# Fourier stages of a two-block kernel: the context's output product placed ahead of the latents', and half of the latents' gate product moved to GpSimd

## The chip, the cores and the metric

The kernel runs on one core of a Trainium2 chip, as one launch. The metric is the device time in microseconds (us), the median over several runs. Engines are named as the profile names them: PE is TensorE (PEld its weight loads), DVE is VectorE, ACT is ScalarE, POOL is GpSimd, SP is SyncE. L3534 is line 3534 of the kernel before.

## The reference

Two transformer-like blocks follow each other on 1024 latent positions and 256 context positions of width 1024. The first (latent attention, a chunkwise mLSTM, a mixture of 16 experts) isn't touched. The second has two layers; each projects its input into parts, runs attention, a Fourier branch, a convolution and a pooling branch, and projects the concatenation with `w_out`. The Fourier branch is:

```python
def _fourier_branch(u, z, w_fourier):
    b, n, _ = u.shape
    uf = u.astype(jnp.float32).reshape(b, n, F_HEADS, F_DIM)      # F_HEADS = 4, F_DIM = 64
    y = jnp.fft.fftn(uf, axes=(1, 3), norm='ortho').real.reshape(b, n, W_F).astype(u.dtype)
    return jax.nn.silu(z) * (y @ w_fourier)                       # W_F = 256
```

In the first layer it is computed for the latents (n = 1024) and for the context (n = 256). In the second layer only the latents' result is needed.

## The kernel before, in words

`layer` (L3723 on) is called for l = 0 and 1. Each layer projects its input, runs attention, then `fourier` (L3386 on, called once per layer), then `project_out`. Everything lies with the 128 partitions as channels and the positions along the row: `g.parts` holds the projected parts, and `g.o[j]`, j = 0 and 1, the two groups of 128 output channels of the Fourier branch. A row has the 256 context positions first and the 1024 latent ones behind them.

The transform along the positions uses symmetry. The input is folded into a sum and a difference of its two halves (`fold`, L3495), turned by TensorE's transposes (L3424), multiplied with a cosine and a sine table (`transform`, L3433), and then multiplied with the combined head transform and `w_fourier` (`w2`). This last stage is called `leave` on TensorE and on VectorE. For each j it gives an even and an odd part, of `half` columns each (512 for the latents, 128 for the context); position t is even plus odd, position n - t is even minus odd. The middle position has products of its own, of one column each (`middle`, and the first loop of `leave`).

There are no planners here: each engine runs a list written out by hand, with semaphores between the lists, within one block (L3394). All engines meet at a barrier at the block's end, before `project_out` starts. The lists before the change, from the point that the change touches:

- TensorE (L3452 to L3472): latents turned and transformed (cosines, `middle`, sines); in layer 0 the context turned and transformed (L3459 to L3464); waits for the latents' spectrum (`cos_out`, `sin_out`, `mid_done`); `leave` of the latents (L3468), which raises `out_full` once per j; in layer 0 waits for the context's spectrum (`cos_out` 3, `mid_done` 2) and `leave` of the context (L3472), which raises `out_full` to 3 and 4.
- ScalarE: copies of the sines' spectrum (L3484), then the odd part of each j out of PSUM (L3487), which raises `odd_done`.
- VectorE: in layer 0 the context's spectrum (`spectra`, L3521), then `leave` of the latents for j = 0 and 1, then of the context for j = 0 and 1. One `leave` is five steps: the middle column (L3526), the odd part (a wait for ScalarE, or for the context a copy, L3530), even plus odd (L3531), even minus odd written backwards (L3532), and the product of the whole row with the gate `z` (L3534). The helper `Steps` lets VectorE wait for each of its own steps before the next.
- GpSimd: four small copies in layer 0, two in layer 1 (L3403), and nothing behind them in this block.
- SyncE: one load of `w_out` (L3397).

`project_out` then begins with ScalarE's rounding of `g.o` and of the weights (L3620, L3625), VectorE's rests (L3660, L3679) and TensorE's products (L156 to L158).

The lines of VectorE's `leave` that the change alters:

```python
dve.wait_ge(out_full, n + 1)
...
    dve.wait_ge(odd_done, n + 1)
...
step(dve.tensor_tensor(dst[:, c0:c0 + 2 * half], dst[:, c0:c0 + 2 * half], z, ALU.mult))
```

Of the kernel before, what the change touches and what calls it, by code (L numbers as in the profile page):

```python
# [11 lines left out]
ALU = mybir.AluOpType  # L12
# [4 lines left out]
P = 128  # L17
BANK = 512
D = 1024
KD = D // P  # L20
N_LAT, N_CTX = 1024, 256
# [2645 lines left out]
Q_AT, K_AT, V_AT, UF_AT, ZF_AT, ZA_AT, N_PARTS = 0, 2, 3, 4, 6, 8, 10  # L2667
# [701 lines left out]
def fourier(nc, g, l, streams):  # L3369

    with Phase(nc, f"f{l}", g.carry) as ph:
# [4 lines left out]
        mid, mid_c = ph.sb("mid", [P, 2, 2]), ph.sb("mid_c", [P, 2, 2])  # L3376
        ab = ph.sb("ab", [P, 2, 2, BANK])
        ab_c = ph.sb("ab_c", [P, 2, 2, P])
        odd, odd_c = ph.sb("odd", [P, 2, BANK]), ph.sb("odd_c", [P, 2, P])
        w2 = ph.sb("w2", [P, 2, 2, 2 * P])  # L3380
        w2_c = ph.sb("w2_c", [P, 2, 2, 2 * P])
        A = ph.ps("a", [P, 4, BANK])
        B = ph.ps("b", [P, 4, BANK])
        names = ("w_full", "w_free", "folded", "turn_full", "even_turned", "odd_turned", "spectrum", "cos_out", "sin_out",
                 "out_full", "odd_done", "dve_step", "mid_done", "first_done")
        (w_full, w_free, folded, turn_full, even_turned, odd_turned, spectrum, cos_out, sin_out, out_full, odd_done,  # L3386
         dve_step, mid_done, first_done) = (ph.sem(n) for n in names)


        work = [(N_CTX, BANK, fold, turned, ab, odd, w2, mid, 0)]  # L3390
        if len(streams) == 2:
            work.append((0, P, fold_c, turned_c, ab_c, odd_c, w2_c, mid_c, 1))

        with nc.Block(no_gpsimd_drain=True) as block:  # L3394
# [4 lines left out]
            @block.gpsimd  # L3399
            def _(pool):  # L3400
                for c0, half, fo, *_ in work:
                    for s in range(2):
                        ins = pool.tensor_copy(fo[:, s, :, 0:1], g.parts[:, UF_AT:UF_AT + 2, c0:c0 + 1])  # L3403
                    ins.then_inc(first_done, 1)

            @block.tensor
            def _(pe):
                pe.wait_ge(g.four_in, 16 * g.n_four)
                for n, (*_, w, _, i) in enumerate(work):
                    for s in range(2):  # L3410
                        for k in range(2):
                            mm = accumulate(nc, B[:, 2 * i + s, k * 2 * P:(k + 1) * 2 * P],
                                            [(g.small[:, i, s, :], g.wf[:, k, :])])
                    mm.then_inc(w_full, 1)

                def turn(c0, half, fo, dst):
                    for s in range(2):
                        pe.wait_ge(folded, 2 * (0 if half == BANK else 1) + s + 1)
                        pe.wait_ge(first_done, 1 if half == BANK else 2)
                        for f in range(2):  # L3420
                            for k in range(half // P):
                                bank = A[:, 2 * s + f, k * P:(k + 1) * P] if half == BANK else \
                                    A[:, 0, (2 * s + f) * P:(2 * s + f + 1) * P]
                                mm = pe.transpose(bank, fo[:, s, f, k * P:(k + 1) * P], g.ident[:])  # L3424
                            if half == BANK:
                                mm.then_inc(turn_full, 1)
                    if half != BANK:
                        mm.then_inc(turn_full, 1)

                def transform(half, tn, table, s, out):  # L3430
                    for f in range(2):
                        for k in range(half // P):
                            mm = nc.tensor.matmul(out(s, f), tn[:, s, f, k * P:(k + 1) * P], table[:, s, k, 0:half],  # L3433
                                                  start=k == 0, stop=k == half // P - 1)
                    return mm

                def middle(half, tn, out):
                    for f in range(2):
                        mm = accumulate(nc, out[:, f:f + 1], [(tn[:, 0, f, k * P:(k + 1) * P], g.alt[:, BANK:BANK + 1])
                                                              for k in range(half // P)])  # L3440
                    return mm

                def leave(half, a, m, w, out, mid_at):
                    for j in range(2):
                        accumulate(nc, mid_at[:, 2 + j:3 + j], [(w[:, 0, f, j * P:(j + 1) * P], m[:, f, 0:1])
                                                               for f in range(2)])
                    for j in range(2):
                        for s in range(2):
                            mm = accumulate(nc, out(j, s), [(w[:, s, f, j * P:(j + 1) * P], a[:, f, s, :]) for f in range(2)])
                        mm.then_inc(out_full, 1)  # L3450

                turn(N_CTX, BANK, fold, turned)  # L3452
                pe.wait_ge(w_free, len(work))
                pe.wait_ge(even_turned, 2)
                transform(BANK, turned, g.dft, 0, lambda s, f: B[:, 2 * f + s, :])
                middle(BANK, turned, A[:, 1, 0:4]).then_inc(spectrum, 1)
                pe.wait_ge(odd_turned, 2)
                transform(BANK, turned, g.dft, 1, lambda s, f: B[:, 2 * f + s, :]).then_inc(spectrum, 1)
                if len(work) == 2:  # L3459
                    turn(0, P, fold_c, turned_c)  # L3460
                    pe.wait_ge(even_turned, 3)
                    for s in range(2):
                        transform(P, turned_c, g.dft_c, s, lambda s, f: A[:, 2, (2 * f + s) * P:(2 * f + s + 1) * P])
                    middle(P, turned_c, A[:, 3, 0:4]).then_inc(spectrum, 1)  # L3464
                pe.wait_ge(cos_out, 2)
                pe.wait_ge(sin_out, 2)
                pe.wait_ge(mid_done, 1)
                leave(BANK, ab, mid, w2, lambda j, s: B[:, 2 * j + s, :], A[:, 1, 0:4])  # L3468
                if len(work) == 2:
                    pe.wait_ge(cos_out, 3)  # L3470
                    pe.wait_ge(mid_done, 2)
                    leave(P, ab_c, mid_c, w2_c, lambda j, s: A[:, 0, (2 * j + s) * P:(2 * j + s + 1) * P], A[:, 3, 0:4])  # L3472

            @block.scalar
            def _(act):
                for n, (*_, w, _, i) in enumerate(work):
                    act.wait_ge(w_full, n + 1)
                    act.activation(w[:].rearrange("p s k n -> p s (k n)"), B[:, 2 * i:2 * i + 2, :], ACT.Copy).then_inc(w_free, 1)
                for f in range(2):
                    act.wait_ge(turn_full, 3 + f)  # L3480
                    act.activation(turned[:, 1, f, :], A[:, 2 + f, :], ACT.Copy).then_inc(odd_turned, 1)
                act.wait_ge(spectrum, 2)
                for f in range(2):
                    act.activation(ab[:, f, 1, :], B[:, 2 * f + 1, :], ACT.Copy).then_inc(sin_out, 1)  # L3484
                for j in range(2):
                    act.wait_ge(out_full, j + 1)
                    act.activation(odd[:, j, :], B[:, 2 * j + 1, :], ACT.Copy).then_inc(odd_done, 1)  # L3487

            @block.vector
            def _(dve):  # L3490
                step = Steps(dve, dve_step)
# [31 lines left out]
                def leave(j, c0, half, even, od, mid_at, n):  # L3523
                    dst, z = g.o[j], g.parts[:, ZF_AT + j, c0:c0 + 2 * half]
                    dve.wait_ge(out_full, n + 1)
                    step(dve.tensor_copy(dst[:, c0 + half:c0 + half + 1], mid_at[:, 2 + j:3 + j]))  # L3526
                    if half == BANK:
                        dve.wait_ge(odd_done, n + 1)
                    else:
                        step(dve.tensor_copy(od[:, j, :], A[:, 0, (2 * j + 1) * P:(2 * j + 2) * P]))  # L3530
                    step(dve.tensor_tensor(dst[:, c0:c0 + half], even, od[:, j, :], ALU.add))  # L3531
                    step(dve.tensor_tensor(back(dst[:, c0 + 2 * half - 1:c0 + 2 * half], half - 1), even[:, 1:half],  # L3532
                                           od[:, j, 1:half], ALU.subtract))
                    step(dve.tensor_tensor(dst[:, c0:c0 + 2 * half], dst[:, c0:c0 + 2 * half], z, ALU.mult))  # L3534

                for j in range(2):
                    leave(j, N_CTX, BANK, B[:, 2 * j, :], odd, A[:, 1, 0:4], j)
                if len(work) == 2:
                    for j in range(2):
                        leave(j, 0, P, A[:, 0, 2 * j * P:(2 * j + 1) * P], odd_c, A[:, 3, 0:4], 3)  # L3540


def project_out(nc, g, l, jobs, normed=None):
# [360 lines left out]
```

## Time and profile before

| | before |
|---|---|
| median of 3 runs | 3502.72 us (3501.15 to 3504.55) |
| the profiled execution's own time | 3500.76 us |
| its span | 3498.9 us |
| granted clock of TensorE, mean over the span | 0.955 of full |
| TensorE busy | 3196.7 us (91%) |
| VectorE busy | 1868.3 us (53%) |
| ScalarE busy | 1438.1 us (41%) |
| GpSimd busy | 664.2 us (19%) |

The span is one profiled execution from its first to its last instruction; the execution's own time has 1.9 us more around it and is 1.96 us under the median. Busy shares are averages over stages with different limits, so a stage is read by its own rows: a row of the timeline gives the start and the duration of an instruction or of a run of equal ones, and in brackets how long the engine stood idle before it and what released it. "PEclk" is the granted TensorE clock as a share of full speed: 1.00 is 2.4 GHz, 0.50 is 1.2 GHz. The Fourier block of layer 0 runs from 2772.15 to 2813.04 us of the span, that of layer 1 from 3365.24 to 3399.79 us.

### The profile page before, as it was taken

The page shows a single profiled execution, that of the slowest core. Times are in us where ns is not written, and L with a number is a line of the kernel's source. Part 1 is how long each engine was busy: PE and PEld are TensorE (multiplying, and loading weights), DVE is VectorE, ACT ScalarE, POOL GpSimd, SP SyncE. Part 2 cuts the span into 40 slices and gives each one's busy share as a digit, 9 for nine tenths or more (in the row PEclk, how much of TensorE's full clock was granted, in tenths as well). Part 3 has the DMA queues.
Part 4 walks back from the last instruction along what each step waited for, and adds up shares of the span by engine and source line. Part 5 has one row for each costly group of instructions (what it writes and reads, how often), then busy time and mean ns, then how long its engine had stood idle before and what let it go on. Part 6 is the DMA issues. An engine that isn't in the chain of part 4 may idle for free. (4 is left out here: it accounts for less than half of the span.)

```text
span 3498.9 us, 43016 instructions
## 1 busy us (share of the span) xinstructions
PE 3196.7 (91%) x17109; PEld 2584.6 (74%) x17109; DVE 1868.3 (53%) x2542; ACT 1438.1 (41%) x2001; POOL 664.2 (19%) x445
## 2 busy tenths in 40 slices
PE   7989998999999799794999999689998997999989
PEld 3867776778778677683778788578887776887867
DVE  4357875444434344556788888543516543153643
ACT  4222222333334344442677777441117534212740
POOL 1200001012111155300455555320000003000000
PEclk7999999999999899896999999899999997999999
DMA  6427665001000132324999999521101124211012
GB/s 202 118 58 236 191 191 168 31 24 45 24 27 24 50 119 69 133 91 188 350 380 387 384 383 381 190 79 50 34 19 36 49 102 169 61 43 49 8 73 84
DMA packets 245424, 463.37 MB, mean 132 GB/s; under 512 B 23647, under 2 KB 135384, under 8 KB 245228
## 3 DMA queue, kind: packets, MB, share of 16 engines
q1 hardware_dynamic: 227368, 401.70, 32.7%
q0 software_dynamic: 15264, 57.70, 4.9%
q8 instruction: 141, 2.31, 0.3%
q10 hardware_dynamic: 2596, 1.20, 0.1%
q14 instruction: 55, 0.45, 0.0%
HBM read 405.34 MB, written 55.22 MB: 132 GB/s over the span
## 5 line engine op out<-in xcount | busy, mean ns | idle before, releaser
L2617 DVE TENSOR_TENSOR exp_wl<-wts_raw,exp_wh 128x2048 fp32r<-128x2048 f32 x144 | 394.3, 2772 | 106.2 <-ACT exp_wh L2577 106.2
L2577 ACT ACTIVATE exp_wh<-wts_raw 128x2048 fp32r<-128x2048 f32 x192 | 368.0, 1919 | 196.4 <-PE exp_gate L2506 65.0
L2797 PE MATMUL pr_ps<-l_h_high,pr_wh 128*128 128x512 f32 (+1 forms) x896 | 334.5, 373 | 0.0
L2798 PE MATMUL pr_ps<-l_h_low,pr_wh 128*128 128x512 f32 (+1 forms) x896 | 329.4, 368 | 0.0
L2799 PE MATMUL pr_ps<-l_h_high,pr_wl 128*128 128x512 f32 (+1 forms) x896 | 328.9, 367 | 0.0
L2476 POOL TENSOR_TENSOR exp_wl<-wts_raw,exp_wh 128x2048 fp32r<-128x2048 f32 x48 | 229.2, 4776 | 265.8 <-ACT exp_wh L2577 265.8
L878 PE MATMUL in_ps<-iw_h_high,in_wh 128*128 128x512 f32 (+1 forms) x696 | 269.6, 387 | 0.0
L879 PE MATMUL in_ps<-iw_h_low,in_wh 128*128 128x512 f32 (+1 forms) x696 | 265.0, 381 | 0.0
L880 PE MATMUL in_ps<-iw_h_high,in_wl 128*128 128x512 f32 (+1 forms) x696 | 264.5, 380 | 0.0
L2971 DVE TENSOR_TENSOR pr_wl<-two_raw,pr_wh 128x512 fp32r<-128x512 f32 x84 | 57.7, 691 | 333.2 <-ACT pr_wh L2877 331.9
L1107 DVE SCALAR_TENSOR_TENSOR g_scratch<-g_scratch,g_c 128x512 f32<-128x512 f32 x240 | 181.3, 783 | 27.6 <-DVE g_scratch L1107 12.6
L2797 PEld LDWEIGHTS pr_ps<-l_h_high,pr_wh 128*128 128x128 f32 x896 | 169.4, 189 | 30.4 <-issue 2.4
L2798 PEld LDWEIGHTS pr_ps<-l_h_low,pr_wh 128*128 128x128 f32 x896 | 169.4, 189 | 29.8 <-issue 2.4
L2799 PEld LDWEIGHTS pr_ps<-l_h_high,pr_wl 128*128 128x128 f32 x896 | 169.2, 189 | 28.2
L1506 DVE TENSOR_REDUCE att_st<-att_sc 128x1 f32<-128x1280 f32 x64 | 95.4, 1491 | 173.2 <-PE att_sc L145 173.1
L878 PEld LDWEIGHTS in_ps<-iw_h_high,in_wh 128*128 128x128 f32 x696 | 133.2, 191 | 37.0 <-issue 12.8
L2877 ACT ACTIVATE pr_wh<-two_raw 128x512 fp32r<-128x512 f32 x88 | 55.3, 629 | 252.1 <-PE pr_ps L2799 252.1
L1481 ACT ACTIVATE att_pT<-att_tb 128x512 f32<-128x512 f32 x128 | 76.4, 598 | 193.6 <-PE att_tb L1392 193.6
L145 PE MATMUL att_tb<-att_pT,att_v 128*128 128x128 f32 x1280 | 154.7, 276 | 0.8 <-DVE att_pT L1560 0.8
L880 PEld LDWEIGHTS in_ps<-iw_h_high,in_wl 128*128 128x128 f32 x696 | 132.8, 191 | 25.1
L879 PEld LDWEIGHTS in_ps<-iw_h_low,in_wh 128*128 128x128 f32 x696 | 133.1, 191 | 24.7 <-issue 0.8
L145 PEld LDWEIGHTS att_tb<-att_pT,att_v 128*128 128x128 f32 x1280 | 149.3, 193 | 1.0 <-issue 1.0
(522 smaller groups left out, 7146.8 us busy)
## 6 DMA issues: line engine op xcount, KB each, us to landing
wts_raw<-in_w_e_gate SPq DMA_DIRECT2D x64, 1024.0 KB, 9.9
wts_raw<-in_w_e_up SPq DMA_DIRECT2D x64, 1024.0 KB, 9.4
wts_raw<-in_w_e_down SPq DMA_DIRECT2D x64, 1024.0 KB, 7.9
g_scratch<-in_w_mod SPq DMA_DIRECT2D x80, 512.0 KB, 4.7
two_raw<-in_w_in SPq DMA_DIRECT2D x84, 256.0 KB, 3.0
iw_raw<-in_w_in SPq DMA_DIRECT2D x74, 256.0 KB, 4.7
mod_w<-in_w_mod SPq DMA_DIRECT2D x4, 2048.0 KB, 11.8
wo_w<-in_w_out SPq DMA_DIRECT2D x2, 4096.0 KB, 12.7
```

Source lines behind the costliest of these rows:

```text
L145: mm = nc.tensor.matmul(out, lhsT, rhs, start=n == 0, stop=n == last)
L878: nc.tensor.matmul(out, wh[:, slot, k, :], hi, start=h == 0 and k == 0, stop=False)
L879: nc.tensor.matmul(out, wh[:, slot, k, :], lw, start=False, stop=False)
L880: mm = nc.tensor.matmul(out, wl[:, slot, k, :], hi, start=False, stop=h == 1 and k == KH - 1)
L1107: ins = dve.scalar_tensor_tensor(a, mw[:, u % QUARTERS, k, :], g.c2[:, blk, 2 * q + k, s:s + 1], bias[:] if q == 0 and k == 0 else a, ALU. ...
L1506: dve.tensor_reduce(st[:, t % 2, 0:1], sc[:, t % 2].rearrange("p b n -> p (b n)")[:, 0:N_ALL], AX.X, ALU.max).then_inc(maxed, 1)
L2476: pool.tensor_tensor(wl[:, POOL_SLOT], raw[:, m % RAW_RING], wh[:, POOL_SLOT].bitcast(F32), ALU.subtract).then_inc(low_pool, 1)
L2577: act.activation(wh[:, m % RING], raw[:, m % RAW_RING], ACT.Copy).then_inc(high, 1)
L2617: dve.tensor_tensor(wl[:, m % RING], raw[:, m % RAW_RING], wh[:, m % RING].bitcast(F32), ALU.subtract).then_inc(low, 1)
L2797: nc.tensor.matmul(out, wh[:, slot, k, :], hi, start=h == 0 and k == 0, stop=False)
L2798: nc.tensor.matmul(out, wh[:, slot, k, :], lw, start=False, stop=False)
L2799: mm = nc.tensor.matmul(out, wl[:, slot, k, :], hi, start=False, stop=h == 1 and k == KH - 1)
```

## The change

TensorE does the context's `leave` before the latents'. VectorE follows in the same order, and the counts of `out_full` follow: `LAT_OUT` is 2 in layer 0 and 0 in layer 1. For the latents, VectorE no longer waits for its own sum (even plus odd), which raises a new semaphore `even_half` instead; GpSimd waits for it and multiplies the lower 512 columns with their gate. VectorE multiplies only the upper 512. GpSimd waits for its two products before it reaches the block's end. The second layer has no context work, so there only the split of the product differs.

```diff
+        LAT_OUT = 2 * (len(streams) - 1)
...
             @block.gpsimd
...
+                for j in range(2):
+                    pool.wait_ge(even_half, j + 1)
+                    cols = slice(N_CTX, N_CTX + BANK)
+                    pool.tensor_tensor(g.o[j][:, cols], g.o[j][:, cols], g.parts[:, ZF_AT + j, cols], ALU.mult).then_inc(gated_half, 1)
+                pool.wait_ge(gated_half, 2)
...
             @block.tensor
...
                 pe.wait_ge(mid_done, 1)
-                leave(BANK, ab, mid, w2, lambda j, s: B[:, 2 * j + s, :], A[:, 1, 0:4])
                 if len(work) == 2:
                     pe.wait_ge(cos_out, 3)
                     pe.wait_ge(mid_done, 2)
                     leave(P, ab_c, mid_c, w2_c, lambda j, s: A[:, 0, (2 * j + s) * P:(2 * j + s + 1) * P], A[:, 3, 0:4])
+                leave(BANK, ab, mid, w2, lambda j, s: B[:, 2 * j + s, :], A[:, 1, 0:4])
...
             @block.scalar
...
-                    act.wait_ge(out_full, j + 1)
+                    act.wait_ge(out_full, LAT_OUT + j + 1)
...
             @block.vector
...
                     if half == BANK:
-                        dve.wait_ge(odd_done, n + 1)
+                        dve.wait_ge(odd_done, j + 1)
+                        dve.tensor_tensor(dst[:, c0:c0 + half], even, od[:, j, :], ALU.add).then_inc(even_half, 1)
                     else:
                         step(dve.tensor_copy(od[:, j, :], A[:, 0, (2 * j + 1) * P:(2 * j + 2) * P]))
-                    step(dve.tensor_tensor(dst[:, c0:c0 + half], even, od[:, j, :], ALU.add))
+                        step(dve.tensor_tensor(dst[:, c0:c0 + half], even, od[:, j, :], ALU.add))
...
-                    step(dve.tensor_tensor(dst[:, c0:c0 + 2 * half], dst[:, c0:c0 + 2 * half], z, ALU.mult))
-
-                for j in range(2):
-                    leave(j, N_CTX, BANK, B[:, 2 * j, :], odd, A[:, 1, 0:4], j)
+                    if half == BANK:
+                        step(dve.tensor_tensor(dst[:, c0 + half:c0 + 2 * half], dst[:, c0 + half:c0 + 2 * half], z[:, half:], ALU.mult))
+                    else:
+                        step(dve.tensor_tensor(dst[:, c0:c0 + 2 * half], dst[:, c0:c0 + 2 * half], z, ALU.mult))
+
                 if len(work) == 2:
                     for j in range(2):
-                        leave(j, 0, P, A[:, 0, 2 * j * P:(2 * j + 1) * P], odd_c, A[:, 3, 0:4], 3)
+                        leave(j, 0, P, A[:, 0, 2 * j * P:(2 * j + 1) * P], odd_c, A[:, 3, 0:4], 1)
+                for j in range(2):
+                    leave(j, N_CTX, BANK, B[:, 2 * j, :], odd, A[:, 1, 0:4], LAT_OUT + j)
```

## Rows read from the trace of the kernel before

**Rows 1.** The page: busy time and share of each engine over the span.
```profile
PE 3196.7 (91%) x17109; PEld 2584.6 (74%) x17109; DVE 1868.3 (53%) x2542; ACT 1438.1 (41%) x2001; POOL 664.2 (19%) x445
```

**Rows 2.** Windows over the two Fourier blocks: length, busy per engine, PEclk, DMA.
```profile
2772.15:2813.04 40.89, 35.37 (x144) 22.26 (x144) 15.92 (x32) 5.42 (x8) 2.56 (x4) 0.96 0.27 103
3365.24:3399.79 34.55, 29.16 (x96) 15.47 (x96) 10.66 (x15) 4.39 (x7) 1.31 (x2) 0.95 0.31 121
```

**Rows 3.** Timeline, layer 0, end of its Fourier block: start, duration, engine, line, what.
```profile
2795.71 0.69 DVE L3519 COPY f_turned_c<-f_a 128x512 f32<-128x512 f32 x1 [5.94 <-PE f_a L3424]
...
2796.46 1.16 PE L3433 MATMUL f_a<-ft_dft_c,f_turned_c 128*128 128x128 f32 x8 [0.78 <-DVE f_turned_c L3519]
...
2797.82 1.03 PE L145 MATMUL f_a<-f_mid,f_w 128*128 128x1 f32 x8
...
2798.71 7.11 PE L145 MATMUL f_b<-f_ab,f_w 128*128 128x512 f32 x16
2798.86 0.15 DVE L3512 TENSOR_TENSOR f_mid_c<-f_a,l_parts 128x2 f32<-128x2 f32 x1
...
2805.66 0.95 PE L145 MATMUL f_a<-f_mid_c,f_w_c 128*128 128x1 f32 x8
...
2805.86 0.60 ACT L3487 ACTIVATE f_odd<-f_b 128x512 f32<-128x512 f32 x1 [2.84 <-PE f_b L145]
...
2806.45 1.87 PEld L145 LDWEIGHTS f_a<-f_ab_c,f_w_c 128*128 128x128 f32 x16
...
2808.01 1.23 DVE L3534 TENSOR_TENSOR l_o_low<-l_o_low,l_parts 128x1024 f32<-128x1024 f32 x1
...
2812.06 0.42 DVE L3534 TENSOR_TENSOR l_o_low<-l_o_low,l_parts 128x256 f32<-128x256 f32 x1
2813.04 0.81 SPq L3577 DMA_DIRECT2D po_gate<-g_modrow  x2
```

**Rows 4.** Timeline, layer 1, the last steps of its Fourier block (j = 1).
```profile
3395.86 0.60 ACT L3487 ACTIVATE f_odd<-f_b 128x512 f32<-128x512 f32 x1 [2.84 <-PE f_b L145]
...
3396.56 0.69 DVE L3531 TENSOR_TENSOR l_o_low<-f_b,f_odd 128x512 f32<-128x512 f32 x1 [0.47 <-ACT f_odd L3487]
3397.29 0.69 DVE L3532 TENSOR_TENSOR l_o_low<-f_b,f_odd 128x511 f32<-128x511 f32 x1
3398.01 1.23 DVE L3534 TENSOR_TENSOR l_o_low<-l_o_low,l_parts 128x1024 f32<-128x1024 f32 x1
```

**Rows 5.** Groups of instructions: count, busy, mean ns of one, idle time before.
```profile
L1866 POOL TENSOR_TENSOR g_hs<-g_hs,mls_ho 128x256 f32<-128x256 f32 x32 | 23.3, 727 | 32.9 <-ACT mls_ho L1982 32.9
L2100 POOL TENSOR_TENSOR mw_hn<-mw_hn,g_yT 128x1024 f32<-128x1024 f32 x4 | 9.4, 2354 | 19.8 <-DVE mw_hn L2138 19.8
L2142 DVE TENSOR_TENSOR mw_hn<-mw_hn,g_yT 128x1024 f32<-128x1024 f32 x4 | 8.6, 2160 | 0.1
L2971 DVE TENSOR_TENSOR pr_wl<-two_raw,pr_wh 128x512 fp32r<-128x512 f32 x84 | 57.7, 691 | 333.2 <-ACT pr_wh L2877 331.9
```

**Rows 6.** Timelines of POOL and DVE in the first block's readout.
```profile
1469.45 2.38 POOL L2100 TENSOR_TENSOR mw_hn<-mw_hn,g_yT 128x1024 f32<-128x1024 f32 x1 [2.35 <-DVE mw_hn L2138]
...
1468.10 2.46 DVE L2138 SCALAR_TENSOR_TENSOR mw_hn<-rdo_tp,g_pa,rdo_s 128x1024 f32<-128x1024 f32 x2
1470.60 2.31 DVE L2142 TENSOR_TENSOR mw_hn<-mw_hn,g_yT 128x1024 f32<-128x1024 f32 x1
```

**Rows 7.** PE by windows around two gaps: length, PE busy, PEclk, DMA.
```profile
2796.45:2798.70 2.25, 2.24 (x20) 1.00 0.03 7
...
3384.92:3386.13 1.21, 0.00 (x0) 1.00 0.00 0
3386.13:3387.00 0.87, 0.87 (x8) 1.00 0.00 0
3387.00:3390.50 3.50, 3.50 (x7) 0.52 0.00 0
```

**Rows 8.** Timeline, layer 1, the latents' output product on PE.
```profile
3387.02 8.81 PE L145 MATMUL f_b<-f_ab,f_w 128*128 128x512 f32 x16
```

More of the change, by code:

```diff
@@ L3387, in fourier @@
          dve_step, mid_done, first_done) = (ph.sem(n) for n in names)
+        even_half, gated_half = ph.sem("even_half"), ph.sem("gated_half")
+        LAT_OUT = 2 * (len(streams) - 1)
         work = [(N_CTX, BANK, fold, turned, ab, odd, w2, mid, 0)]
```

## The prediction

> **What bounds the kernel now.** I began with the page's busy shares: TensorE works 91% of the span, VectorE 53%, GpSimd 19% [rows 1]. The kernel as a whole is TensorE's, but each layer's Fourier stages are a block of their own with a barrier behind it, so the change can be worth only what it moves that barrier. The windows over the two blocks say how much there is to move: 40.89 us in layer 0 and 34.55 us in layer 1, 75.4 us of 3498.9, and TensorE is busy in 64.5 of them [rows 2]. The chain of waits on the page follows only the last products of the output projection and never reaches these blocks, so I read their ends from the timeline.
>
> Layer 0 ends on VectorE. The latents' last product (L3534) ends at 2808.01 + 1.23 = 2809.24; the context's ten steps follow at once and end at 2812.06 + 0.42 = 2812.48, and 0.56 us later, behind the barrier, the next phase issues its first load at 2813.04 [rows 3]. TensorE issued its last product near 2808.32 and is not what is waited for. So 3.24 us of context work stand bare at the end. Layer 1 ends on VectorE too: for j = 1 ScalarE copies the odd part from 3395.86, VectorE adds, subtracts, and multiplies the row until 3399.24 [rows 4].
>
> **The change, part by part, in layer 0.** The starting point is 2812.48, the end of VectorE's list.
>
> 1. *The context's ten steps leave the tail:* -3.24 us, from above. They run beside TensorE's latent product instead. That cover is long enough: the one-column products from 2797.82 to 2798.71 and half of the 7.11 us behind them make 4.4 us until the first latent output, against 3.24 us of steps [rows 3].
>
> 2. *TensorE reaches the latents later.* Before, it went on to the latents' one-column products at 2797.82 without a stop, since their operands had been there for long. Now it must first have the context's spectrum, whose last part VectorE writes from 2798.86 to 2799.01 [rows 3]. A release by VectorE reaches TensorE in 0.06 us (the copy from 2795.71 ends at 2796.40, the products start at 2796.46), so it stands still until about 2799.07. Behind this wait stands all that TensorE has left, the context's and the latents' output alike, and ScalarE's and VectorE's last steps wait for those. Then come the context's products: from 2805.66 to the end of their weight loads at 2806.45 + 1.87 = 2808.32 is 2.66 us [rows 3]. The latents start at 2801.73 instead of 2797.82: +3.91 us on everything behind.
>
> So the exchange of order by itself costs: 3.91 of TensorE's time goes in front of the last latent output, 3.24 of VectorE's goes from behind it, +0.67 us.
>
> 3. *The half product on GpSimd.* For j = 1 the tail is, in layer 1's times: the sum ends at 3397.25, the difference at 3397.98, the product over 1024 columns at 3399.24 [rows 4]. GpSimd can start once the sum is there. The trace shows no 512-column product on it, but 256 columns take 727 ns and 1024 take 2354 [rows 5], 2.12 ns a column between them, so 1.27 us. Its wake-up is 0.12 us: VectorE's two L2138 begin at 1468.10 and take 1.23 each, and GpSimd starts at 1469.45 behind the first [rows 6]. It would work from 3397.37 to 3398.64. VectorE's own half takes 0.69 us undisturbed [rows 5], from 3398.01 to 3398.70. Read so, 0.54 us are gained per layer.
>
> But the two overlap, and both read two SBUF operands. Rows 6 hold just this case. GpSimd's product runs 1469.45 to 1471.83; VectorE's product of 1024 columns, 1.23 us elsewhere [rows 4], starts at 1470.60 and takes 2.31, ending 1.08 us behind GpSimd. VectorE stands nearly still until GpSimd is through, and only some 0.15 us (1.23 - 1.08) of its start-up overlap. The four products of that line have a mean of 2160 ns [rows 5], so the pair is no exception. L2138, which reads PSUM and one SBUF tensor, is not slowed (2.46 for two), so the difference L3532 should not be either. For 512 columns VectorE then ends 0.69 - 0.15 = 0.54 us behind GpSimd: 3398.64 + 0.54 = 3399.18, against 3399.24. The bounds are -0.54 and, if it waited in full, +0.09; I take -0.06 by rows 6, the same pair of operations. For j = 0 the same delay is covered by the wait for j = 1's odd part. The wait dropped between sum and difference had 0.03 us of room, nothing.
>
> The Trainium skill would have GpSimd finish a little earlier: its page GPSIMD Engine Reference, section 3.1, gives about 2.6 cycles an element at 1.2 GHz, an estimate of 1.11 us for 512 columns; by that page's figure each layer would end 0.16 us sooner. The rows have durations for the same operation, and they are used.
>
> 4. *TensorE's clock.* TensorE already stood 0.78 us before 2796.46 [rows 3], works on small products, and its clock stays at 1.00, 2.4 GHz [rows 7]. Part 2 adds a second gap, from about 2797.95 to 2799.07, 1.1 us, and puts one-column products on both sides of it and 128-column ones behind. The nearest row is layer 1: a gap of 1.21 us, 0.87 us of one-column products, and then the clock is at 0.52 on average (1.2 GHz) for 3.5 us [rows 7]. There 16 products of 512 columns took 8.81 us [rows 8] against 7.11 in layer 0 [rows 3]: 1.70 us. Between nothing and 1.70 I take 1.70, because layer 0 would have two gaps and small work around both, more than layer 1 had. It lies on the path, since VectorE waits for TensorE in full. A doubled spell, 3.4 us, is the far bound.
>
> **The sum.** Layer 0: +0.67 - 0.06 + 1.70 = +2.31. Layer 1: no context, no new wait on TensorE, -0.06. Together +2.25, put at +2.3 us. The DMA queues keep their order (SP's load of the weights is long landed), GpSimd's list held nothing behind its copies, and its new closing wait ends before VectorE does. The barrier's 0.56 us stays. Against the profiled execution's 3500.76 this gives 3503.1; the median lies 1.96 higher, so 3502.72 + 2.3 = **3505.0 us**. A difference under 0.2%, 7.0 us, can't be told from none.
>
> **The rivals.**
>
> *A. As summed,* +2.3 us: 0.55.
>
> *B. The clock holds.* For it: 0.78 us of gap did not lower it in layer 0, and no new gap is as long as layer 1's 1.21. Against it: there are now two, with little between. The time is 3502.72 + 0.6 = 3503.3: 0.22. The Trainium skill speaks for this one: in TensorE: Matmul & The Clock Gate, Part 1, the clock falls back after an idle spell. Rows 7 show it fall where TensorE was only partly idle, so I don't give it more.
>
> *C. Both halves truly run side by side,* since VectorE here writes other columns and the tensors lie elsewhere. Then each layer gains 0.54 in place of 0.06: 3505.0 - 1.0 = 3504.0, or, with the clock held too, 3502.3. For it, the mean of the four pairs, 2.16 us, is under the 2.31 of the pair shown, so not all were slowed alike [rows 5, 6]; against it, even the mean is 0.93 over the 1.23 alone. 0.08.
>
> *D. Two slow spells in place of one,* or one at the output projection's start that falls later: +4.0, 3506.7: 0.10. The clock is already low there in the trace, so mostly it only shifts.
>
> *E. The slow clock does not come back in this block.* Its place is layer 0 from the context's output on. All that TensorE does there doubles: about 1.9 for the context, 7.1 for the latents, so +9 and the 0.6 of the order, 3512: slower by over 0.2%. It decides once the clock stays at 0.50 for 12.8 us on end, as 6.4 us have to be lost besides the 0.6. Against it: in layer 1 it came back after 3.5 us of dense work [rows 7]. 0.03.
>
> *F. The order does not change in effect:* TensorE's wait for the context's spectrum is met late enough that all shifts by more, or the products overlap as before. Bounded by 1 us either way, 3502 to 3504: 0.02.
>
> **How the numbers follow.** A, B, C, D and F lie within 0.2%: 0.97, less a hundredth for drift that no case here makes, 0.96 for no difference, 0.03 for slower (E), 0.01 for faster. The range takes the lowest of C, -0.4, less the 1.6 by which the fastest run lies under the median, so 3500.7, rounded to 3500.5; at the top D's +4.0 and the 1.8 of the slowest run, 3508.5. Only E lies outside.
>
> **What would show each step.** In the profile after: in layer 0 the context's products ahead of the 16 of 512 columns, a gap of TensorE near 1.1 us before them released by VectorE's `f_mid_c`, and the last odd copy at about 2809.8, or 2811.5 with the slow clock. A window from 2799 to 2804 should show the clock near 0.5. POOL should have two products of 1.27 us per layer, and VectorE's last upper product should take about 1.2 us in place of 0.69, ending 0.54 behind POOL. Layer 1's block should keep its length within 0.1 us. An upper product of 0.69 beside POOL proves C; a clock of 1.00 throughout proves B. The prediction is wrong as a whole if the block of layer 0 grows by over 6 us or the stretches outside the two blocks move.

## The result, and the profile after

| | before | after |
|---|---|---|
| median of 12 runs each | 3504.53 us (3501.15 to 3510.61) | 3512.09 us (3504.62 to 3515.47) |
| ratio after to before | | 1.0019, 95% interval 1.001 to 1.0027 |
| span of the profiled execution | 3498.9 us | 3510.1 us |
| Fourier block, layer 0 | 40.89 us | 44.77 us |
| Fourier block, layer 1 | 34.55 us | 34.47 us |

The change makes the kernel slower by 0.19%, 3.5 to 9.5 us by the interval. Forecast were +2.3 us and at most 3508.5. Part of the miss is the starting point: with nine more runs of the kernel before its median is 3504.5, 1.8 us over the three that were shown.

The two Fourier blocks of the profiled execution, by windows (busy per engine, PEclk, DMA), against [rows 2]; by its first instructions the second block runs from 3376.27 to 3410.74:

```profile
2776.15:2820.91 44.76, 38.67 (x144) 24.94 (x144) 15.82 (x32) 5.41 (x8) 5.10 (x6) 0.89 0.24 94
3376.35:3410.83 34.48, 29.13 (x96) 15.42 (x96) 10.52 (x15) 4.46 (x8) 3.78 (x4) 0.92 0.32 122
```

TensorE is busy 3.3 us longer in layer 0 with the same 144 records, and its clock is 0.89 instead of 0.96. The block's own length understates the loss: the slow clock at its start in [rows 2], some 3.4 us long, happened not to be there this time. So I use the **end piece** from here on: from the start of the copy f_turned_c, which comes after all that and ahead of all that changed, to the next phase's first load. It was 17.33 us (2795.71 to 2813.04, [rows 3]) and is 22.90 (2798.01 to 2820.91): **+5.57 us**.

The timeline of that stretch, after (start, duration, engine, line), against [rows 3]:

```profile
2801.16 0.15 DVE L3519 TENSOR_TENSOR f_mid_c<-f_a,l_parts 128x2 f32<-128x2 f32 x1
2801.50 1.84 PE L145 MATMUL f_a<-f_mid_c,f_w_c 128*128 128x1 f32 x8 [1.24 <-DVE f_mid_c L3519]
2803.20 3.76 PE L145 MATMUL f_a<-f_ab_c,f_w_c 128*128 128x128 f32 x16
2806.75 1.71 PE L145 MATMUL f_a<-f_mid,f_w 128*128 128x1 f32 x8
...
2808.32 8.72 PE L145 MATMUL f_b<-f_ab,f_w 128*128 128x512 f32 x16
...
2809.79 0.43 DVE L3545 TENSOR_TENSOR l_o_low<-l_o_low,l_parts 128x256 f32<-128x256 f32 x1
...
2817.07 0.60 ACT L3494 ACTIVATE f_odd<-f_b 128x512 f32<-128x512 f32 x1 [2.84 <-PE f_b L145]
...
2817.77 0.69 DVE L3536 TENSOR_TENSOR l_o_low<-f_b,f_odd 128x512 f32<-128x512 f32 x1 [0.47 <-ACT f_odd L3494]
2818.38 0.68 DVE L3540 TENSOR_TENSOR l_o_low<-f_b,f_odd 128x511 f32<-128x511 f32 x1
2818.54 1.26 POOL L3410 TENSOR_TENSOR l_o_low<-l_o_low,l_parts 128x512 f32<-128x512 f32 x1 [2.16 <-DVE l_o_low L3536]
2819.09 1.26 DVE L3543 TENSOR_TENSOR l_o_low<-l_o_low,l_parts 128x512 f32<-128x512 f32 x1
2820.91 0.82 SPq L3588 DMA_DIRECT2D po_gate<-g_modrow  x2
```

The order of work is the one that was predicted, the gap is there and is released by f_mid_c, the context's ten steps are done by 2810.22, long ahead of the latents' second odd part at 2817.07. But every product of TensorE behind the gap is slow: the one-column ones take 1.84 and 1.71 us where they took 0.95 and 1.03, the context's sixteen 3.76 for 2.03, the latents' sixteen 8.72 for 7.11. (The counts are the profile's records; an f32 product leaves two of them.) The same stretch by windows of TensorE (length, busy, PEclk, DMA), against [rows 7]:

```profile
2798.76:2800.20 1.44, 1.44 (x12) 1.00 0.00 0
2800.20:2801.50 1.30, 0.06 (x2) 0.93 0.00 0
2801.50:2804.70 3.20, 3.20 (x15) 0.50 0.02 5
2804.70:2808.10 3.40, 3.40 (x18) 0.50 0.00 0
2808.10:2811.50 3.40, 3.40 (x6) 0.50 0.00 0
2811.50:2817.00 5.50, 5.50 (x13) 0.99 0.00 0
```

The clock falls near the end of the gap and stays at 1.2 GHz for 10.2 us, where layer 1's fall lasts 3.5 [rows 7]. What remained open was which part of the change does it, whether the standstill or the small products bring the clock down, and how much of the 5.57 us, or of the 3.2 us that the stretch between the two blocks is longer in this execution (555.4 against 552.2), comes again.

### The profile page after: what moved, and what is told of

Read it like the earlier page. It is cut to its first block and busy times, and to the rows that moved or that the text cites. A ratio compares the mean times of both kernels' runs of the same rounds, so it can differ in the third digit from the quotient of the medians.

```text
span 3510.1 us, 43022 instructions
## 1 busy us (share of the span) xinstructions
PE 3205.9 (91%) x17109; PEld 2591.4 (74%) x17109; DVE 1867.8 (53%) x2542; ACT 1437.8 (41%) x2001; POOL 669.1 (19%) x449
```

## The experiments

**The order alone.** The changed kernel with the gate product whole on VectorE again:

```diff
-                    pool.wait_ge(even_half, j + 1)
-                    ...
-                pool.wait_ge(gated_half, 2)
...
-                        dve.tensor_tensor(dst[:, c0:c0 + half], even, od[:, j, :], ALU.add).then_inc(even_half, 1)
+                        step(dve.tensor_tensor(dst[:, c0:c0 + half], even, od[:, j, :], ALU.add))
...
+                    step(dve.tensor_tensor(dst[:, c0:c0 + 2 * half], dst[:, c0:c0 + 2 * half], z, ALU.mult))
```

> The new order of the two output products alone, the gate product whole on VectorE again. Measured on the end piece of layer 0: from the start of the copy f_turned_c to the first load of the next phase, 17.33 us before (2795.71 to 2813.04) and 22.90 after the change (2798.01 to 2820.91). Theory (the loss is the order's, by the new wait and the slow clock behind it): the end piece is 22.9 to 23.1 us, PEclk near 0.50 from the gap until well into the latents' product, the run 4 to 7 us slower than before. Rival (the GpSimd products cause the loss, by port contention or their place in the barrier): the end piece falls back to 17.3 to 18.2 us and the run is within 2 us of before. Second rival (the slow spell's length is chance): an end piece between, near 19.7 us, with one short spell of the slow clock.

Measured: ratio 1.0014 (1.0004 to 1.0023), end piece 2797.46 to 2820.53, 23.07 us. Its timeline:

```profile
2797.46 0.69 DVE L3520 COPY f_turned_c<-f_a 128x512 f32<-128x512 f32 x1 [5.94 <-PE f_a L3425]
...
2800.94 1.82 PE L145 MATMUL f_a<-f_mid_c,f_w_c 128*128 128x1 f32 x8 [1.23 <-DVE f_mid_c L3513]
2802.63 3.76 PE L145 MATMUL f_a<-f_ab_c,f_w_c 128*128 128x128 f32 x16
...
2820.53 0.81 SPq L3579 DMA_DIRECT2D po_gate<-g_modrow  x2
```

The whole loss is the order's. With the split it is 0.17 us less.

**The split alone.** TensorE, ScalarE and VectorE in the order of before, GpSimd with its half:

```diff
-        LAT_OUT = 2 * (len(streams) - 1)
+        LAT_OUT = 0
...
+                leave(BANK, ab, mid, w2, lambda j, s: B[:, 2 * j + s, :], A[:, 1, 0:4])
                 if len(work) == 2:
                     ...
-                leave(BANK, ab, mid, w2, lambda j, s: B[:, 2 * j + s, :], A[:, 1, 0:4])
...
```

> The half product on GpSimd alone, TensorE and VectorE in the order of before. Theory: the two half products run one behind the other on the shared access to SBUF, so layer 1's block keeps its length (34.5 us, before 34.55) and layer 0's end piece stays at 17.2 to 17.4 us (before 17.33): VectorE's upper half takes 1.2 to 1.3 us beside POOL instead of 0.69. The run is within 3 us of before. Rival (side by side): the halves take 0.69 and 1.27 us and layer 1's block shortens by 0.5 us. Rival (the split causes the loss of the change): the run is 5 us or more slower.

Measured: ratio 0.9999 (0.9987 to 1.001), end piece 2798.64 to 2815.89, 17.25 us, layer 1's block 34.46, as expected. In the timeline of its DVE and POOL in layer 0:

```profile
2810.81 1.27 DVE L3543 TENSOR_TENSOR l_o_low<-l_o_low,l_parts 128x512 f32<-128x512 f32 x1
...
2810.26 1.27 POOL L3410 TENSOR_TENSOR l_o_low<-l_o_low,l_parts 128x512 f32<-128x512 f32 x1 [2.16 <-DVE l_o_low L3536]
```

VectorE's 512 columns take 1.27 us and end 0.55 behind GpSimd's (2812.08 against 2811.53). They overlap for 0.72 us, and VectorE's product takes 0.58 us more than its 0.69 alone, so it hardly advances while GpSimd works. Moving half of the row saves about 0.1 us a layer and costs nothing.

**The gap filled.** The changed kernel with three products whose result nobody reads, into a bank that the latents' output overwrites later:

```diff
                 if len(work) == 2:
+                    for _ in range(3):
+                        nc.tensor.matmul(B[:, 0, :], w2[:, 0, 0, 0:P], ab[:, 0, 0, :], start=True, stop=True)
                     pe.wait_ge(cos_out, 3)
```

> The changed kernel with three products of 512 columns (1.3 us of work whose result is never read) on TensorE in the gap before it waits for the context's spectrum. The rest is as changed. Theory (the clock falls because the stretch is sparse, and every later small product runs at half speed): with the gap filled PEclk stays at 1.00 through the context's and the latents' output; the end piece is 22.9 less 4.9, that is 18.0 us (17.7 to 18.3), 0.7 longer than before. Rival (the small products of the context by themselves keep the clock down, gap or no gap): the clock still falls and the end piece stays at 20 us or more.

Measured: ratio 1.0017 (1.0005 to 1.0029), end piece 2797.78 to 2817.02, 19.24 us. The clock stays at 1.00 until 2815.8, when TensorE is already done. The piece is 1.2 us over the expected 18.0 because I mis-sized the filling: one such product is two passes of 0.43 us, each a record of its own, so three take 2.57 us and not 1.3, and the surplus lies on the path. Less the 1.3 us by which the filling is longer than the gap it is 17.9, the theory's number. The whole-run ratio is higher than a piece that is 1.9 us longer explains. That called for the two repeats below.

**The gap alone.** The kernel before, its order kept, with the wait ahead of the latents:

```diff
+                if len(work) == 2:
+                    pe.wait_ge(cos_out, 3)
+                    pe.wait_ge(mid_done, 2)
                 leave(BANK, ab, mid, w2, lambda j, s: B[:, 2 * j + s, :], A[:, 1, 0:4])
```

> The kernel before with one thing added: TensorE waits for the context's spectrum (mid_done 2) ahead of the latents' output too, the order otherwise as before. So the gap of 1.2 us is there, but dense products of 512 columns follow it. Theory (the gap lowers the clock, and dense work behind it brings it back after one spell, as in layer 1): end piece 17.33 + 1.25 + 1.7 = 20.3 us, PEclk 0.5 for about 3.5 us. Rival (the gap alone holds the clock down for 10 us): 17.33 + 1.25 + 3.5 or more, 22 us and up. Rival (the gap does nothing, the small products do): 18.6 us, clock 1.00.

Measured: ratio 1.0023 (1.0014 to 1.0033), end piece 22.05 us. TensorE by windows:

```profile
2801.46:2802.80 1.34, 0.11 (x1) 1.00 0.00 0
2802.80:2804.40 1.60, 1.60 (x9) 0.54 0.00 0
2804.40:2809.70 5.30, 5.30 (x8) 0.50 0.01 3
2809.70:2814.00 4.30, 4.30 (x12) 1.00 0.00 0
```

My number, 20.3, was wrong, and it is the same error as in the prediction. The wait itself costs 1.4 us (the first product behind it starts 3.48 us after the copy f_turned_c, against 2.11 before); the slow clock another 3.3 to 3.4, not 1.7. It stayed low for 6.8 us although sixteen dense products stood right behind the one-column ones; the rival of 22 us and up has the piece's number, but not the 10 us of slow clock that it asked for. So one added wait, with no other change, brings 4.7 of the change's 5.6 us. Its whole run is slower by more than that, 0.23% or some 8 us; in its one profile 3.9 us of it lie between the two blocks (556.1 us against 552.2).

**Two versions in which the wait is met in time,** so that TensorE doesn't stand. In the first, the context is turned ahead of the latents' sines, and its output goes between the latents' two:

```diff
+                if len(work) == 2:
+                    turn(0, P, fold_c, turned_c)
                 pe.wait_ge(odd_turned, 2)
                 transform(BANK, turned, g.dft, 1, lambda s, f: B[:, 2 * f + s, :]).then_inc(spectrum, 1)
...
-                leave(BANK, ab, mid, w2, lambda j, s: B[:, 2 * j + s, :], A[:, 1, 0:4])
+                leave(*lat, js=(0,))
                 ...
+                leave(*lat, js=(1,))
```

> A version without the bare wait, the gate product whole on VectorE: TensorE turns the context ahead of the latents' sines, transforms it behind them, and does the latents' output for j = 0, then the context's, then the latents' for j = 1. Measured from the start of layer 0's sines (L3433's second run of 16 products, 2788.13 before) to the first load of the next phase: 24.91 us before (2813.04). Theory (the wait and the sparse stretch behind it are what cost; dense work in the gap keeps the clock at 1.00): 0.6 us of gap goes, the context's ten steps and its products hide, so 23.0 to 23.6 us, PEclk 1.00 to the end, the whole run 1 to 2 us faster than before, within what a measurement can tell. Rival (small products by themselves bring the clock down): 25 us or more with a slow stretch.

In the second, the context is also transformed ahead of the sines, and its output is whole ahead of the latents':

```diff
+                if len(work) == 2:
+                    turn(0, P, fold_c, turned_c)
                 middle(BANK, turned, A[:, 1, 0:4]).then_inc(spectrum, 1)
                 pe.wait_ge(odd_turned, 2)
-                transform(BANK, turned, g.dft, 1, lambda s, f: B[:, 2 * f + s, :]).then_inc(spectrum, 1)
                 if len(work) == 2:
-                    turn(0, P, fold_c, turned_c)
                     ...
                     middle(P, turned_c, A[:, 3, 0:4]).then_inc(spectrum, 1)
+                transform(BANK, turned, g.dft, 1, lambda s, f: B[:, 2 * f + s, :]).then_inc(spectrum, 1)
+                if len(work) == 2:
+                    pe.wait_ge(cos_out, 3)
+                    pe.wait_ge(mid_done, 2)
+                    leave(P, ab_c, mid_c, w2_c, lambda j, s: A[:, 0, (2 * j + s) * P:(2 * j + s + 1) * P], A[:, 3, 0:4])
                 ...
```

> The changed order without its wait: the context is turned and transformed ahead of the latents' sines, so its spectrum is ready when the sines end, and its output is multiplied ahead of the latents' while ScalarE copies the sines. Gate product whole on VectorE. Theory: TensorE never stands, though it has small products in two runs (about 3.5 us ahead of the sines, 3.6 us behind them). Counted from the end of the cosines (2786.42 before, to 2813.04: 26.62 us), 24.7 to 25.2 us with the clock at 1.00. Rival (what lowers the clock is the share of small products, not a standstill): the clock falls in one of the two runs and the piece is 26.5 us or more.

Measured for the first: 2788.97 to 2811.91, 22.94 us, just under the expected 23.0 to 23.6, against 24.91 before; ratio 1.0005 (0.9996 to 1.0014), so the 1 to 2 us expected of the whole run don't show. From the end of the cosines it is 25.12 against 26.62. For the second: 2791.70 to 2816.70, 25.00 us, against 26.62; ratio 1.0 (0.9991 to 1.001). The second's products, from its timeline:

```profile
2791.70 0.60 PE L3424 MATMUL f_a<-g_ident,f_fold_c 128*128 128x128 f32 x4
2792.14 1.84 PE L145 MATMUL f_a<-ft_alt,f_turned 128*128 128x1 f32 x16
2793.84 1.14 PE L3433 MATMUL f_a<-ft_dft_c,f_turned_c 128*128 128x128 f32 x8
2794.82 0.50 PE L145 MATMUL f_a<-ft_alt,f_turned_c 128*128 128x1 f32 x4
2795.18 7.11 PE L3433 MATMUL f_b<-ft_dft,f_turned 128*128 128x512 f32 x16
2802.14 0.95 PE L145 MATMUL f_a<-f_mid_c,f_w_c 128*128 128x1 f32 x8
2802.95 2.03 PE L145 MATMUL f_a<-f_ab_c,f_w_c 128*128 128x128 f32 x16
2804.81 0.95 PE L145 MATMUL f_a<-f_mid,f_w 128*128 128x1 f32 x8
2805.62 7.11 PE L145 MATMUL f_b<-f_ab,f_w 128*128 128x512 f32 x16
```

The second run of small products, 3.6 us from 2802.14 on, is the very one that stands behind the gap in the changed kernel, and another of 3.5 us stands 7 us ahead of it. Without the standstill all of them go at full speed. They aren't wholly the changed kernel's surroundings, though: there the context's transform lies right before the gap, and here dense sines lie between. The two versions take 1.5 and 1.6 us out of the block in one profile each. Whole runs can't show that, so neither is shown to beat the kernel before.

**Both kernels once more,** unchanged.

> The kernel before once more, for the spread between executions. Theory: the end piece of layer 0 is 17.3 us again (17.2 to 17.5), layer 1's block 34.55, and what differs between executions lies outside: the start of layer 0's block (2772.15 in the one profile, 2775.6 to 2777.4 in the five variants) comes out anywhere from 2771 to 2778. Rival (the variants are systematically late upstream): it starts again near 2772. Rival (the clock's fall is chance): the end piece differs by 1.7 us or more.

> The changed kernel once more. Theory: the end piece is again 22 to 23.5 us with the clock at 0.50 for 7 us or more from the gap on, layer 1's block 34.45 to 34.5. Rival (the long slow spell was chance): the end piece is under 20.5 us.

Measured: end pieces 17.33 and 22.81 us, layer 1's blocks 34.56 and 34.46. After's clock was low for 10.2 us again. The end piece repeats within 0.1 us, so the loss in it is no chance. What scatters lies outside: the kernel before started its layer 0 block at 2776.93 this time, so the variants are not late upstream, and the changed kernel started it at 2773.20. In the four profiles with the unfilled gap (the changed kernel's two, the order alone, the gap alone) the gap lies at 2.25 to 3.49 us from the start of the copy f_turned_c, and the clock falls at 3.14 to 3.59.

**The smallest filling,** one product in place of three, and the first filling once more.

```diff
-                    for _ in range(3):
+                    for _ in range(1):
                         nc.tensor.matmul(B[:, 0, :], w2[:, 0, 0, 0:P], ab[:, 0, 0, :], start=True, stop=True)
```

> As fill_gap, with one product of 512 columns (0.86 us, by fill_gap's six records in 2.57 us) in place of three, so that TensorE still stands for some 0.35 us. Theory (a standstill over 1 us beside small products is what tips the clock): it stays at 1.00, the end piece is 22.85 - 4.9 = 17.9 to 18.3 us, and this is the changed order at its own price, 0.6 to 0.9 us over before's 17.33. Rival (any standstill there is enough): the clock falls and the end piece is 21 us or more.

> fill_gap once more, one execution. Theory: end piece 19.24 us again (17.9 to 18.0 plus 1.2 that the second and third filling product take beyond the gap), clock 1.00 up to the block's end. Rival (in fill_gap the clock held by chance): a slow stretch in the piece, 21 us or more.

Measured with one product: ratio 1.0001 (0.999 to 1.0012), end piece 17.98 us. The three repeat with 19.25. The timeline of TensorE with one product, and its windows:

```profile
2798.88 1.10 PE L3477 MATMUL f_b<-f_ab,f_w 128*128 128x512 f32 x2
2800.20 1.02 PE L145 MATMUL f_a<-f_mid_c,f_w_c 128*128 128x1 f32 x8 [0.22 <-DVE f_mid_c L3521]
2801.09 2.03 PE L145 MATMUL f_a<-f_ab_c,f_w_c 128*128 128x128 f32 x16
```

```profile
2797.51:2799.98 2.47, 2.46 (x14) 1.00 0.00 0
2799.98:2800.20 0.22, 0.00 (x1) 1.00 0.00 0
2800.20:2803.70 3.50, 3.50 (x32) 1.00 0.02 5
2803.70:2810.60 6.90, 6.90 (x18) 1.00 0.00 0
```

This settles what brings the loss. One product with no use, 0.86 us of work in a gap of 1.24, takes 4.9 us off the end piece (22.90 to 17.98), and the changed kernel is no longer told from the one before. TensorE still stands for 0.22 us of the gap. How much of it has to be filled isn't shown, nor whether shorter or longer gaps act alike; the piece with one filling product rests on one profile.

| kernel | end piece, us | clock low in it while TensorE works, us | ratio to before |
|---|---|---|---|
| before, twice | 17.33, 17.33 | 0 | |
| split only | 17.25 | 0 | 0.9999 |
| changed, one filling product | 17.98 | 0 | 1.0001 |
| changed, three filling products, twice | 19.24, 19.25 | 0 | 1.0017 |
| before with the wait | 22.05 | 6.8 | 1.0023 |
| changed, twice | 22.90, 22.81 | 10.2 | 1.0019 |
| order only | 23.07 | 10.2 | 1.0014 |

The end piece stops at the block's end, and what lies behind it isn't the same in all profiles. TensorE's clock is low at the start of the output projection in every profile. That stretch lasts 6.8 us in both kernels and in both parts of the change alone, but 10.2 us in the three profiles with a filling, in the gap alone and in the second of the two versions above. The first stretches of the projection, TensorE by windows, before and with one filling product:

```profile
2813.04:2820.50 7.46, 3.94 (x9) 0.54 0.80 274
```

```profile
2814.75:2823.80 9.05, 5.53 (x13) 0.50 0.69 233
```

Thirteen slow products stand there in place of nine, an estimate of 0.8 us, as one takes 0.43 us at 0.50 and 0.23 at 1.00. That is part of what the ratio 1.0017 holds beyond the end piece. It isn't the filling's own doing alone, as two kernels without one have it too.

## Why the prediction was wrong

*Parts 1 and 2, the exchange of the two orders, +0.67 us, and part 3, -0.06:* right, and now measured at full clock. With one filling product the end piece is 17.98 against 17.33, +0.65 where the sum of layer 0's other terms gave +0.61. The gap was 1.24 us, 0.12 more than the forecast 1.12: TensorE needed 0.19 us from the end of f_mid_c, at 2801.31, to its first product, and not 0.06.

*Part 3 in itself:* right to some hundredths. GpSimd's product takes 1.26 to 1.27 us (forecast 1.27 by the two sizes around it) and VectorE's half ends 0.55 behind it (forecast 0.54). Layer 1's block is 0.09 us shorter, forecast 0.06. The two rows from another stage, the same pair of operations [rows 6], carried this. The Trainium skill (GPSIMD Engine Reference, section 8, Key points) names contention with VectorE instructions that read two SBUF inputs and gives no price for it; the trace agrees, and the price here is 0.58 us on a product of 0.69.

*Part 4, the slow clock, +1.70 us:* this is the step that failed. Its direction and its place were right. Its size was 4.9 us (22.90 less 17.98). I took layer 1's fall as the price, and it was the lowest case: the clock fell there only 1.0 us behind the gap's end, when the one-column products were over and dense work stood next, and it was back after 3.5 us. In the changed layer 0, 0.8 us of one-column products at full speed, the context's sixteen of 128 columns and 0.9 us more of one-column ones stand behind the gap. At half speed these alone fill 2801.50 to 2808.32, 6.8 us, all of it at 0.50, and only 3.2 us of the dense products later does the clock rise. The far bound that I gave, a doubled spell of 3.4 us, was used up by the gap alone with dense work behind it, and with the small work behind it 4.9 us were lost. The prediction had seen both the gap and the small products, and priced only the gap.

*The rivals.* A (+2.3) and D (+4.0) had the right mechanism and too short a spell. E, that the clock does not come back in this block, was nearer to what happened than its chance of 0.03: it stayed low for 10.2 of the 12.8 us that E asked for. That E's 3512 us is the measured median is luck: E added 9.6 us in layer 0, and the end piece grew by 5.6; the rest is the base and what lies outside the blocks. B, a held clock, is refuted for the changed kernel and is what one filling product makes true. C, halves side by side, is refuted by VectorE's 1.27 us. F, no change in effect, is refuted by the new order of TensorE's products and the 5.6 us.

*The range and the chances.* The sum of the measured parts is +5.57 in layer 0 and -0.09 in layer 1, 5.5 us, which lies within the interval of the whole runs (3.5 to 9.5) and under their medians' 7.6. With 3504.5 as the base it gives 3510.0. The forecast counted 3.4 us of spread from three runs; twelve spread over 9.5. It also took every difference under 7.0 us for none, and gave that 0.96. Twelve runs of each kernel tell 0.19% from none: the interval, 0.10 to 0.27%, leaves zero out.

The 3.2 us between the two blocks are one of the prediction's own signs of being wrong as a whole, a stretch outside that moves. They aren't tied to the change: they came in the split alone (555.4) and not in the changed kernel's second profile (552.4). I can't show that the chance of such a stretch is the same in both kernels; with two profiles of each that stays open, above all as neither of the kernel before had it. So does the rest of the ratios of the three filling products (1.0017) and of the gap alone (1.0023), which are more than their pieces explain.

## What to carry to other kernels

Before an order of work is changed, look at what TensorE does in the microseconds around a new wait, and not only at the wait's length: a gap of 1.2 us among small products cost 4.9 us in slow products behind it, four times itself. If the wait can't be avoided, a product without use in the gap cost nothing in the stage itself, and one that fills two thirds of it was enough here. A stage of some 40 us in a kernel of 3500 should be judged by a piece of the timeline between two fixed instructions, which repeated within 0.1 us where whole runs scatter by 10. The stage behind it has to be looked at too, since the slow clock there can last longer.

## What the runs showed of the hardware that was not expected

How long the clock stays low went with what TensorE did once it had fallen. It was low for 3.4 us in layer 1, with dense work from the fall on, in all twelve profiles; for 6.8 us in layer 0 with 1.5 us of one-column products and then dense ones (the gap alone, one profile); and for 10.2 us with 6.8 us of small products first, in all three profiles of the changed order without a filling. Between the copy f_turned_c and TensorE's last product of the block, the clock never fell where the standstill of 1.2 us was missing (eight profiles). The Trainium skill (TensorE: Matmul & The Clock Gate, Part 1) lets the clock fall after an idle spell; here it fell where TensorE stood for 1.2 us at a time, with work on both sides, and in the stretch that follows with no standstill at all, which that rule doesn't cover.

The scatter of the whole runs has a like cause, at least in part. In layer 1's projection TensorE has 32 records of products of two columns and then six of 512 (f32), without a pause. In the changed kernel's first profile the clock fell there, by windows:

```profile
3034.57:3036.80 2.23, 2.23 (x22) 1.00 0.00 0
3036.80:3043.60 6.80, 6.80 (x20) 0.50 0.00 0
```

In the kernel before they start at 3026.62 and ran at 1.00:

```profile
3024.00:3030.00 6.00, 6.00 (x45) 1.00 0.00 0
3030.00:3036.80 6.80, 6.80 (x28) 1.00 0.42 141
```

Of the twelve profiles taken in all, six show this fall for 6.8 us, 2.1 to 2.6 us behind the first of the two-column products, each with a stretch of 555.4 to 556.4 us between the two blocks, and one for 3.4 us (553.0); the five without it, both of the kernel before and the changed kernel's second among them, have 551.5 to 552.5. So the clock can fall at such small products without any standstill. Whether it does differs from one execution to the next, and what decides it isn't shown.
